# First GEMM of both feed-forward blocks with activations stationary and 512 weight columns moving

## What is computed

```python
def swiglu(h, w_in, w_out):
    a, b = jnp.split(h @ w_in, 2, axis=-1)
    return (jax.nn.silu(a) * b) @ w_out
...
h = modulate(x, norm_ffn1[l], sh1, sc1)
x = x + 0.5 * g1 * swiglu(h, w_ffn1_in[l], w_ffn1_out[l])
...
h = modulate(x, norm_ffn2[l], sh3, sc3)
x = x + 0.5 * g3 * swiglu(h, w_ffn2_in[l], w_ffn2_out[l])
```

## Time and profile before

| | |
|---|---|
| median of 3 runs | 2865.64 us |
| lowest and highest | 2865.18, 2868.14 us |
| profiled execution: span | 2863.1 us (no total of its own is listed beside it) |
| TensorE busy, records | 2574.2 us, 20140 |
| VectorE busy | 1781.1 us |
| ScalarE busy | 997.2 us |
| mean granted TensorE clock | 0.938 |
| bytes moved | 567.49 MB, 198 GB/s on average |

### The profile page before, as it was taken

How to read it: one execution, slowest core, us unless ns; L and a number is a source line. 1 busy time by engine, 2 the same in 40 slices (tenths; PEclk the granted TensorE clock), 3 DMA queues, 4 the chain that set the end, 5 groups by cost and what they waited for, 6 DMA issues and landing times. The chain is left out here.

```text
span 2863.1 us, 47785 instructions
## 1 busy us (share of the span) xinstructions
PE 2574.2 (90%) x20140; PEld 2536.1 (89%) x20140; DVE 1781.1 (62%) x1754; ACT 997.2 (35%) x690; POOL 221.1 (8%) x214
## 2 busy tenths in 40 slices
PE   5589989999989788788999988989799999999897
PEld 5589989999989688688899988989699989999897
DVE  5666656767656656888777775656575545444444
ACT  1044433333333322323334443333344333333333
POOL 0010000460000112232400000000000000000000
PEclk6589999999999879889999999999899999999999
DMA  8777767777767552233346655756487645555451
GB/s 297 265 221 264 264 205 240 261 251 263 247 203 246 187 176 89 89 118 103 118 150 213 226 191 190 236 191 246 136 276 252 228 148 194 180 182 185 144 183 70
DMA packets 386137, 567.49 MB, mean 198 GB/s; under 512 B 12709, under 2 KB 209829, under 8 KB 385253
## 3 DMA queue, kind: packets, MB, share of 16 engines
q1 hardware_dynamic: 385332, 560.33, 58.1%
q0 software_dynamic: 688, 5.51, 0.6%
HBM read 561.59 MB, written 4.19 MB: 198 GB/s over the span
## 5 line engine op out<-in xcount | busy, mean ns | idle before, releaser
L264 PE MATMUL gps<-hs,whi 128*128 128x256 f32 x9088 | 1687.8, 288 | 161.9 <-DVE wlo L774 103.8
L264 PEld LDWEIGHTS gps<-hs,whi 128*128 128x128 f32 x9088 | 1446.9, 196 | 174.6 <-DVE wlo L774 107.2
L774 DVE TENSOR_TENSOR wlo<-raw,whi 128x2048 fp32r<-128x2048 f32 x400 | 925.3, 2314 | 858.9 <-ACT whi L520 858.8
L264 PE MATMUL gps<-hs,wlo 128*128 128x256 f32 x4544 | 1301.5, 286 | 0.0
L520 ACT ACTIVATE whi<-raw 128x2048 fp32r<-128x2048 f32 x400 | 765.3, 1914 | 1318.2 <-PE gps L264 1314.9
L264 PEld LDWEIGHTS gps<-hs,wlo 128*128 128x128 f32 x4544 | 888.6, 196 | 0.0
L264 PE MATMUL gps<-ffs,whi 128*128 128x256 f32 x2752 | 506.6, 287 | 27.8 <-DVE ffs L840 23.9
L264 PEld LDWEIGHTS gps<-ffs,whi 128*128 128x128 f32 x2752 | 434.6, 194 | 33.3 <-issue 24.4
L791 DVE SCALAR_TENSOR_TENSOR acc<-raw,cact,acc 128x512 f32<-128x512 f32 x508 | 384.7, 757 | 15.6
L264 PE MATMUL gps<-ffs,wlo 128*128 128x256 f32 x1376 | 392.2, 285 | 0.0
L264 PEld LDWEIGHTS gps<-ffs,wlo 128*128 128x128 f32 x1376 | 267.3, 194 | 0.0
(11 more groups left out here) (216 smaller groups left out, 1328.8 us busy)
## 6 DMA issues: line engine op xcount, KB each, us to landing
raw<-in_w_ffn_in_dram SPq DMA_DIRECT2D x336, 512.0 KB
raw<-in_w_ada_dram SPq DMA_DIRECT2D x144, 1024.0 KB
raw<-in_w_in_dram SPq DMA_DIRECT2D x80, 1024.0 KB
raw<-in_w_ffn_out_dram SPq DMA_DIRECT2D x56, 1024.0 KB
raw<-in_w_ffn_out_dram SPq DMA_DIRECT2D x40, 768.0 KB
raw<-in_w_a_proj_dram SPq DMA_DIRECT2D x16, 1024.0 KB
raw<-in_w_b_glu_dram SPq DMA_DIRECT2D x32, 512.0 KB
raw<-in_w_out_dram SPq DMA_DIRECT2D x16, 1024.0 KB
```

Source lines behind the costliest of these rows:

```text
L264: return pe.matmul(out, lhsT, rhs, start=start, stop=stop, skip_group_check=True)
L774: dve.tensor_tensor(wlo[:, mpos % SPLIT, :, :], raw[:, pos % RING, :, :], whi[:, mpos % SPLIT, :, :].bitcast(F32), ALU.subtract).then_inc( ...
```

## The change

In the phases of the first GEMM (`evac` "pair") the roles are exchanged. A 128-token block of `hs` is stationary and the slab's 512 columns move (`slab_pair`), 24 matmuls a slab, first all for tokens 0 to 127, then all for tokens 128 to 255. The output then has tokens on the partitions, and so have `sil` and `prod`. Since the second GEMM wants features there, `turn` transposes `prod` on TensorE into `mps` (four transposes of 128 x 128, two for the narrow half), between the first and the second token block of the next half's first slab, and ScalarE and VectorE make `ffs` from `mps`. The last turn of a loop (`owed`) falls into the first slab of the second GEMM, whose slabs now wait each for the part of `ffs` that they read. ScalarE has a new wait, `ff_turned`. Transfers, splits, the order on VectorE and the other phases stay.

```diff
--- before.py
+++ after.py
...
@@ -559,13 +559,13 @@
                 out = gps[:, b, :, :]
                 if ph.evac == "pair":
                     act.wait_ge(sem("prod_free"), r.p + i * 2 + g + 1)
-                    act.activation(sil[:, :, :], out[:, 0:2, :], ACT.Silu).then_inc(sem("silu_ready"), 1)
-                    act.wait_ge(psum_free(b), q)
+                    n_cols = COLS // 4 if ph.narrow and g == 1 else COLS // 2
+                    act.activation(sil[:, :, 0:n_cols], out[:, 0:4:2, 0:n_cols], ACT.Silu).then_inc(sem("silu_ready"), 1)
+                    act.wait_ge(sem("ff_turned"), r.pt + i * 2 + g + 1)
                     f = ph.start + i * 2 + g
-                    k = 2
-                    if ph.narrow and g == 1:
-                        k = 1
-                    act.activation(ffs[:, bass.ds(2 * f, k), 0, :], prod[:, 0:k, :], ACT.Copy).then_inc(sem("ff_hi"), 1)
+                    k = n_cols // P
+                    turned = mps[:, g, :].rearrange("p (b s) -> p b s", b=2)
+                    act.activation(ffs[:, bass.ds(2 * f, k), 0, :], turned[:, 0:k, :], ACT.Copy).then_inc(sem("ff_hi"), 1)
                 elif ph.evac == "conv":
                     if i or g:
                         xbc_silu(2 * i + g - 1, q - 1 + g)
@@ -625,6 +625,8 @@
                 r.q += ph.bodies
                 if ph.evac in ("pair", "glu"):
                     r.p += 2 * ph.bodies
+                if ph.evac == "pair":
+                    r.pt += 2 * ph.bodies
 
             def norm(k, last=False):
                 act.wait_ge(sem("x_ready"), 4)
@@ -833,11 +835,14 @@
                 if ph.evac == "pair":
                     p = r.p + i * 2 + g
                     dve.wait_ge(sem("silu_ready"), p + 1)
-                    dve.tensor_tensor(prod[:, :, :], sil[:, :, :], out[:, 2:4, :], ALU.mult).then_inc(psum_free(b), 1)
+                    n_cols = COLS // 4 if ph.narrow and g == 1 else COLS // 2
+                    dve.tensor_tensor(prod[:, :, 0:n_cols], sil[:, :, 0:n_cols], out[:, 1:4:2, 0:n_cols], ALU.mult
+                                      ).then_inc(psum_free(b), 1)
                     dve.wait_ge(sem("ff_hi"), p + 1)
                     f = ph.start + i * 2 + g
-                    k = 1 if ph.narrow and g == 1 else 2
-                    dve.tensor_tensor(ffs[:, bass.ds(2 * f, k), 1, :], prod[:, 0:k, :],
+                    k = n_cols // P
+                    turned = mps[:, g, :].rearrange("p (b s) -> p b s", b=2)
+                    dve.tensor_tensor(ffs[:, bass.ds(2 * f, k), 1, :], turned[:, 0:k, :],
                                       ffs[:, bass.ds(2 * f, k), 0, :].bitcast(F32), ALU.subtract
                                       ).then_inc(sem("prod_free"), 1)
                 elif ph.evac == "resid":
@@ -1190,6 +1195,7 @@
         @block.tensor
         def _(pe):
             r = Run()
+            owed, ff_from = [0], [0]
 
             def ada_end(c, used, fresh=True):
 
@@ -1230,22 +1236,58 @@
                 per, mper = len(ph.stream), 2 * ph.slabs
                 moving = {"h": hs, "ff": ffs, "yb": ybs}[ph.moving]
 
-                if ph.moving == "ff":
-                    pe.wait_ge(sem("prod_free"), r.p + 1)
-                elif ph.name == "w_out":
+                if ph.evac == "pair" and not owed[0]:
+                    ff_from[0] = r.p
+                if ph.name == "w_out":
                     pe.wait_ge(sem("prod_free"), r.p + 1)
                 elif ph.name == "a_proj":
                     pe.wait_ge(sem("y_lo"), 1)
                 elif ph.name == "b_glu":
                     pe.wait_ge(sem("y_lo"), 2)
 
+                def slab_pair(g, s, mp, k0, narrow):
+                    n_cols = COLS // 4 if narrow else COLS // 2
+                    for c in range(2):
+                        tok = slice(P * c, P * c + P)
+                        out = gps[:, g, 2 * c:2 * c + 2, 0:n_cols]
+                        for k in range(ph.chunks[s]):
+                            hi = whi[:, mp % SPLIT, k, :].rearrange("p (h n) -> p h n", h=2)[:, :, 0:n_cols]
+                            lo = wlo[:, mp % SPLIT, k, :].rearrange("p (h n) -> p h n", h=2)[:, :, 0:n_cols]
+                            xh, xl = moving[:, k0 + k, 0, tok], moving[:, k0 + k, 1, tok]
+                            mm(pe, out, xh, hi, k0 + k == 0, False)
+                            mm(pe, out, xh, lo, False, False)
+                            ins = mm(pe, out, xl, hi, False, k0 + k == NT - 1)
+                        yield ins
+
+                def slab_plain(g, s, mp, k0):
+                    for j in range(4):
+                        for k in range(ph.chunks[s]):
+                            hi = whi[:, mp % SPLIT, k, P * j:P * j + P]
+                            lo = wlo[:, mp % SPLIT, k, P * j:P * j + P]
+                            xh, xl = moving[:, k0 + k, 0, :], moving[:, k0 + k, 1, :]
+                            out = gps[:, g, j, :]
+                            mm(pe, out, hi, xh, k0 + k == 0 and j % 2 == 0, False)
+                            mm(pe, out, hi, xl, False, False)
+                            ins = mm(pe, out, lo, xh, False, k0 + k == sum(ph.chunks) - 1)
+                        yield ins
+
+                def turn(g, p, q, blocks):
+                    pe.wait_ge(psum_free(g), q)
+                    pe.wait_ge(sem("prod_free"), p + 1)
+                    for b in range(blocks):
+                        for c in range(2):
+                            ins = pe.transpose(mps[:, g, S * b + P * c:S * b + P * c + P],
+                                               prod[:, c, P * b:P * b + P], ident[:, :])
+                    ins.then_inc(sem("ff_turned"), 1)
+
                 def body(i):
+                    head = isinstance(i, int) and i == 0
                     for g in range(2):
                         if isinstance(i, int) and r.q + i == 0:
                             pass
                         else:
                             pe.wait_ge(psum_free(g), r.q + i)
-                        tiles = [0, 2] if ph.narrow and g == 1 else [0, 1, 2, 3]
+                        narrow = ph.narrow and g == 1
                         for pos, (what, gg, s) in enumerate(ph.stream):
                             if what != "w" or gg != g:
                                 continue
@@ -1254,25 +1296,27 @@
                             k0 = sum(ph.chunks[:s])
                             if ph.moving == "h" and g == 0 and ph.name not in ("a_proj", "w_out"):
                                 pe.wait_ge(sem("h_lo"), 4 * (norms[0] - 1) + s + 1)
-                            for j in tiles:
-                                for k in range(ph.chunks[s]):
-                                    hi = whi[:, mp % SPLIT, k, P * j:P * j + P]
-                                    lo = wlo[:, mp % SPLIT, k, P * j:P * j + P]
-                                    xh, xl = moving[:, k0 + k, 0, :], moving[:, k0 + k, 1, :]
-                                    out = gps[:, g, j, :]
-                                    mm(pe, out, hi, xh, k0 + k == 0 and j % 2 == 0, False)
-                                    mm(pe, out, hi, xl, False, False)
-                                    ins = mm(pe, out, lo, xh, False, k0 + k == sum(ph.chunks) - 1)
-                                if j < 3:
+                            if ph.moving == "ff" and head and g == 0:
+                                pe.wait_ge(sem("prod_free"), ff_from[0] + (k0 + ph.chunks[s] + 1) // 2 + 1)
+                            parts = slab_pair(g, s, mp, k0, narrow) if ph.evac == "pair" else slab_plain(g, s, mp, k0)
+                            for j, ins in enumerate(parts):
+                                if s == 0 and j == 0:
+                                    if ph.evac == "pair" and g == 1:
+                                        turn(0, r.p + 2 * i, r.q + i + 1, 2)
+                                    elif g == 0 and (not head or owed[0]):
+                                        if ph.evac == "pair":
+                                            turn(1, r.p + 2 * i - 1, r.q + i, owed[0] if head else 2)
+                                        elif head:
+                                            turn(1, r.p - 1, r.q, owed[0])
+                                if ph.evac != "pair" and j < 3:
                                     next(side, None)
                             ins.then_inc(slab_done, 1)
                             next(side, None)
                     if ph.ada:
                         ada_end(r.c + i, n0 + i * per + ph.stream.index(("ada", 0, 3)) + 1)
 
-
                 start = 0
-                if r.q == 0:
+                if r.q == 0 or (ph.evac == "pair" and not owed[0]) or ph.moving == "ff":
                     body(0)
                     start = 1
                 if ph.side:
@@ -1285,6 +1329,9 @@
                     body(start)
                 r.q += ph.bodies
                 r.c += ph.ada * ph.bodies
```

(5 more changed lines are left out.)

## The result

| | before | after |
|---|---|---|
| median (lowest to highest) of 4 runs each | 2865.41 (2865.09 to 2868.14) us | 2965.99 (2964.11 to 2969.22) us |
| ratio, 95% interval | | 1.0349 (1.0334 to 1.0364) |
| span of the profiled execution | 2863.1 us | 2964.7 us |
| mean granted TensorE clock | 0.938 | 0.923 |

The change costs 100.6 us; forecast were 60. The time lies in the range (2875 to 2970), near its upper end.

The account below looks back on a forecast made before the run. TensorE, busy 90% of the span, was taken as the bound. Without the clock +16 us, cooling +31 and +14, less 2 at the second GEMM: +59, taken as 60, so 2926 us; range 2875 to 2970.

Parts of the forecast that it names:

- The stall: TensorE waits for the product at turns: 5.6 us (inner, with modulation vectors), 2.5 (without), 1.7 (outer, with); 136 us together.
- The wider matmul's pace: First GEMM: a float32r matmul of 512 moving columns takes 216 ns, so a slab takes 5.18 us, 0.59 less.
- rival 2: The wider matmul is no faster per column: 3012 us at 240 ns, 2966 if today's 13 ns stay; chance 0.12.
- The cooling: Clock drops after 15 stalls of 5.6 us (+31) and two in three of 12 of 2.5 us (+14); second GEMM -2.
- the forecast's sum without the clock: Seams +31, +7 and -2, first halves of the four loops -9, second GEMM's start -11: +16 us.
- The forecast's ada bodies: Loop bodies that compute modulation vectors beside the first GEMM: 50 to 53 us each expected, against 48.56 before.
- The second GEMM's start: TensorE resumes earlier at four starts, saving 2.7 us each: -11 us; waits there shrink to some 3 or 4 us.
- the splits: First GEMM: the third slab's split is ready 0.7 us before it is wanted, so today's stop of about 1.6 us goes.
- the transfers: Same bytes in a body that is no shorter, at 259 GB/s now.
- Rival 1: The clock holds: 2874 us if even long stalls leave it at 2.4 GHz, 2911 if only 2.5 us ones do; chance 0.14.
- Rival 3: At outer seams with modulation vectors, 1.7 us stall plus 0.44 of transposes cools 13 more stretches: +22, 2948 us; chance 0.08.
- Rival 4: Weight load sets a matmul's pace, not its columns: 512 columns in 0.120 us, 2720 us; chance 0.03.

Follow-up runs that it names:

- the filled kernel: The changed kernel with unused 512-column matmuls issued ahead of each turn's wait in the first GEMM: 2927.88 us, 1.0204 of the kernel before.
- the kernel with the product ahead: The changed kernel with VectorE's product ahead of the four accumulations of the modulation slab at inner seams of bodies computing modulation vectors: 2911.47 us, 1.0145 of the kernel before.

## Why the prediction was right in its sign and short in its size

- **The stall.** Right in place, cause and size. Forecast were 5.6, 2.5 and 1.7 us, found are 5.31, 2.29 and 1.33 to 1.40; each a little short, because half a slab takes 2.72 us and not 2.59, and because the last matmul's record runs 0.17 us beyond the next one's start, so that TensorE counts as idle only from there. The total is 140.9 with the starts of the second GEMM and 131.0 without; forecast were 136 without. Two experiments on its two causes, the turn's place and the product's place, took away 120.5 and 54.5 us, and both together 176.6.
- **The wider matmul's pace.** This is the step that failed, a term of the sum that was taken too small. "I take 216 ns" rested on the float32 records, "512 and 1024 ticks plus a few ns". A float32r matmul of 512 columns takes 227: its 213.3 and 13.3 more, the same 13.3 that the 256-column one has (120 less 106.7). 3,576 x 10.7 ns = +38 us. The middle value of rival 2, "if today's 13 ns over the columns' time stay with each", gave 2966, and 2965.99 was measured; but it has the cooling of the forecast in it, which came out somewhat otherwise (below), so that the hit is partly luck. The evidence was there: the row of the same type and form at 256 columns. I gave the weight to a row of the same column count but another type.
- **The cooling.** Forecast 31 + 14 - 2 = 43, found 29 + 10 by the windows, confirmed by the 38 us of the filled kernel. "All long ones, two in three of the plain ones" became all of 15 and six of 12. At the second GEMM all four starts now keep their clock, -8 and not -2; that is partly luck, for behind waits of the same length three of the four cooled in the kernel with the product ahead, and three in the one with filled waits.
- **Not in the sum.** A turn behind a stall that cooled runs cold itself, 0.77 us instead of 0.41, of which some 0.23 lies ahead of the windows, which begin 0.5 us behind the turn's start. That holds for the 15 long stalls, +3; the turns behind the six plain ones took 0.41 us, since there the clock fell later. Two inner ada seams in block 1 stalled 7.9 and 6.5 us, +4. And ahead of the last second GEMM, at 2795.00, TensorE stands for 1.6 us for which the profile names no cause ("issue"), and which the kernel before does not have there, +2.
- **The balance.** 16 (the forecast's sum without the clock) + 38 (pace) + 39 - 8 (clock) + 3 + 4 + 2 = 94, measured 100.6; where the rest lies is open. The ada bodies of block 1's first loop take 55.0 us against 54.35 in block 2, but that is the clock again (0.71 behind their long stalls, 0.77 there), and the 39 hold it. The forecast's ada bodies, 50 to 53, were short by the pace, 168 x 10.7 ns = 1.8 a body.
- **The second GEMM's start, the splits, the transfers** came out nearly as planned: the 23.9 us of waits for `ffs` are gone (9.9 us of waits for the product stand at the four starts in their place), the stops at `wlo` fell from 42 to 31 (106.4 to 81.3 us), and the splits kept up.
- **Rival 1** (the clock holds) fails by the windows. **Rival 3** (transposes count as idling) was not seen: 1.33 us of stall and 0.41 of transposes left the clock at 1.00 at every outer ada seam. The Trainium skill (TensorE: Matmul & The Clock Gate, Part 4: PE-mode transpose), by whose rule transposes are no activity, is neither borne out nor refuted by 1.7 us. **Rival 4** (the load sets the pace) fails by the 227 ns. The Trainium skill (TensorE: Matmul & The Clock Gate, Back-to-back issue gap) has 131 ns for a sustained stream of 512-column matmuls with their loads; the trace has 227, and the measurement decides.

## What to carry to other kernels

A transpose or any other dependent step put into an in-order stream costs whatever its input lacks at that point, so first place it behind the work that its input's latency spans, and move its producer ahead of work that nobody waits for; here these two moves turned +3.5% into -2.8%. Size a new instruction form by the row of the same data type, and keep the fixed part per instruction that this row shows; a change's gain is to be measured against the old form with the same waits taken out, not against the old kernel.

## What the runs showed of the hardware

- A float32r matmul of 256 or 512 moving columns has a fixed 13.3 ns over its columns at 2.4 GHz (256 columns 120 ns, 512 columns 227) and none at 1.2 GHz (512 columns 427 ns, 256 columns 213). The bank written and the operands do not change it (227 and 227 ns), and 64 or 32 stationary columns do not shrink it (229 and 232 ns). It does not carry over to 128 moving columns: these took 110 ns warm and 213 cold, as long cold as 256 columns do, and twice their own time at 1.2 GHz. The float32 records show 216 ns for what would be 512 ticks. The Trainium skill (TensorE: Matmul & The Clock Gate, Part 1, "Wait — 56ns, not 53.3ns?") knows a fixed cost per matmul that only shows when warm, some 2.5 ns; the trace agrees for float32, and has five times that for float32r. What it comes from stays open.
- Back-to-back float32r matmuls of 128 moving columns, once the clock had fallen behind the seam, stayed at 1.2 GHz though TensorE was never idle (213 ns each, clock 0.50 for the 40 us shown). The same slabs with 256 columns, in the change, were warm again some 4 us behind the turn and had one more dip of 3.4 us (from 860 to 884 us).
- In a band the length of a stall does not say whether the clock falls. In the plain bodies, where stalls of 2.29 us come every 25 us, every other one cooled for most of the loop in the change. 3.56 us ahead of the second GEMM's first turn left it at 1.00 in the change and cooled it in the kernel with the product ahead:

```profile
2382.00:2390.00 8.00, 8.00 (x69) 8.00 (x68) 2.15 (x3) 2.51 (x2) 0.00 (x0) 1.00 0.29 100
```

```profile
2328.00:2336.00 8.00, 8.00 (x57) 8.00 (x56) 0.78 (x2) 2.51 (x2) 0.00 (x0) 0.79 0.32 100
```

The first row is of the change, the second of the other kernel, both 8 us from the end of the same turn. With the turns' stalls of 4.9 us and more (48 in the change and four of the other kernels) it always fell, with those of 1.2 to 1.5 us never.
